# Result additions in four pieces and row picks a group ahead, in a two-block transformer kernel

## The reference

```python
gates = jnp.sum(jax.nn.one_hot(eidx, N_EXPERTS, dtype=jnp.float32) * w[..., None], axis=-2)
hg = jnp.einsum('cd,edf->cef', xc, w_eg)
hu = jnp.einsum('cd,edf->cef', xc, w_eu)
a = jax.nn.silu(hg) * hu * gch[..., None]
routed = jnp.einsum('cef,efd->cd', a, w_ed)
shared = (jax.nn.silu(t @ w_sg) * (t @ w_su)) @ w_sd
x = x + gate2 * (routed + shared)
```

## Time and profile before

| | |
|---|---|
| median of 3 runs | 1175.13 us (1171.66 to 1176.56) |
| the profiled execution | 1178.99 us |
| its span | 1177.2 us |
| TensorE busy | 1006.8 us (86%) |
| VectorE busy | 449.6 us (38%) |
| transfers | 376.77 MB, mean 320 GB/s |
| mean granted TensorE clock | 0.931 of full |

### The profile page before, as it was taken

How to read it: one execution, slowest core, us unless ns; L and a number is a source line. 1 busy time by engine, 2 the same in 40 slices (tenths; PEclk the granted TensorE clock), 3 DMA queues, 4 the chain that set the end, 5 groups by cost and what they waited for, 6 DMA issues and landing times. The chain is left out here.

```text
span 1177.2 us, 14285 instructions
## 1 busy us (share of the span) xinstructions
PE 1006.8 (86%) x5213; PEld 573.7 (49%) x5213; DVE 449.6 (38%) x1011; ACT 207.2 (18%) x438; POOL 157.7 (13%) x209
## 2 busy tenths in 40 slices
PE   6999997987977767799999998889999999837286
PEld 3545543444322222345555444858878888403231
DVE  1795272244211110234915116544443433234431
ACT  2204201330111111302624112010111111100000
POOL 0000011100000000000000000045554554221000
PEclk9999998898999999699999998899999999978597
DMA  8552588989799999952598959779999999998886
GB/s 320 207 214 73 197 315 313 358 366 388 304 421 423 422 421 416 345 143 90 200 343 312 360 211 372 283 276 409 375 381 353 357 373 343 377 417 355 364 334 272
DMA packets 71813, 376.77 MB, mean 320 GB/s; under 512 B 20047, under 2 KB 22347, under 8 KB 41883
## 3 DMA queue, kind: packets, MB, share of 16 engines
q1 hardware_dynamic: 58347, 328.54, 71.6%
q0 software_dynamic: 13424, 47.69, 10.5%
HBM read 338.66 MB, written 48.14 MB: 329 GB/s over the span
## 5 line engine op out<-in xcount | busy, mean ns | idle before, releaser
L877 PE MATMUL bank<-wring,hT 128*128 128x512 f32 (+3 forms) x608 | 249.8, 570 | 7.7 <-DVEq L1704 3.8
L877 PEld LDWEIGHTS bank<-wring,hT 128*128 128x128 f32 x608 | 112.9, 198 | 132.5 <-issue 122.0
L1112 PEld LDWEIGHTS bank<-qT,wring 128*128 128x128 f32 x1408 | 158.9, 192 | 5.3 <-issue 4.3
L1112 PE MATMUL bank<-qT,wring 128*128 128x128 f32 x1408 | 159.3, 275 | 0.2 <-DVE qT L2253 0.2
L1040 PE MATMUL bank<-wring,kT 128*32 128x512 f32 x768 | 102.6, 665 | 39.4 <-DMA wring<-in_w_pack 36.9
L1002 PE MATMUL bank<-kT,x 128*128 128x128 f32 x480 | 72.0, 321 | 51.9 <-DVEq L1704 51.5
L1002 PEld LDWEIGHTS bank<-kT,x 128*128 128x128 f32 x480 | 69.3, 234 | 63.0 <-DVEq L1704 55.4
L788 POOL DMA_INDIRECT PRT<-xn_parts_dram,part_now x88 | 89.6, 1019 | 39.0 <-issue 22.7
L1126 PE MATMUL bank<-wring,PRT 128*128 128x512 f32 x176 | 77.7, 593 | 0.9 <-ACT hT L1429 0.7
L1040 PEld LDWEIGHTS bank<-wring,kT 128*32 128x32 f32 x768 | 26.2, 120 | 106.6 <-issue 57.5
L877 PE MATMUL bank<-wring,yT 128*128 128x512 f32 x160 | 70.2, 595 | 0.7 <-ACT yT L1429 0.7
(11 more groups left out here) (368 smaller groups left out, 1005.3 us busy)
## 6 DMA issues: line engine op xcount, KB each, us to landing
wring<-in_w_pack SPq DMA_DIRECT2D x154, 1024.0 KB, 14.6
wring<-in_w_pack SPq DMA_DIRECT2D x22, 2048.0 KB, 8.8
y_dram<-gateB SPq DMA_DIRECT2D x8, 4096.0 KB, 19.5
wring<-in_w_ada POOLq DMA_DIRECT2D x24, 1024.0 KB, 7.3
wring<-in_w_pack SPq DMA_DIRECT2D x32, 512.0 KB, 15.3
wring<-in_pack_z.0 SPq DMA_DIRECT2D x1, 2048.0 KB, 10.9
wring<-in_pack_z.2 SPq DMA_DIRECT2D x1, 2048.0 KB, 17.3
wring<-in_pack_z.3 SPq DMA_DIRECT2D x1, 2048.0 KB, 8.9
```

The costliest lines, as they stand in the source:

```text
L877: mm = nc.tensor.matmul(b[:, 0:n], lhs(k, t), w[:, k, c0:c0 + n], start=(k == 0), stop=(k == nk - 1))
L1112: mm = nc.tensor.matmul(bank[:, s, f * P:(f + 1) * P], item_gate_up(s)[:, k, f * P:(f + 1) * P], xT[:, s, k, :], start=(k == 0), stop=(k = ...
```

## The change

It has four parts. In block two VectorE weighs and picks one group further ahead: `weigh(1)` and `pick(2)` come before the steps, and `step(i)` is now hidden, next_rows, gated_result, `weigh(i+1)`, `pick(i+2)`. The sixteen result additions are cut into four pieces of four, one after each of steps 1, 2 and 3, and the fourth after the loop, ahead of the last group's hidden product; the closing pair of a token half comes with pieces 1 and 3 (counted from 0). Since three steps are now written out, the least number of groups in block two is 5. And on TensorE the last group of each block makes down half 1 and down half 0 one behind the other, then both sums; the other groups keep their order.

```diff
+LEAST_SMALL_QUADS = 5
...
-                    for half in (1, 0):
-                        if half == 0 and last is None:
-                            pe.wait_ge(E(f"moe{n}_quad_rows_copied"), i + 1)
+                    def down(half):
                         if last is not None:
                             pe.wait_ge(E(f"moe{n}_last_loaded{4 + half}"), 64)
...
+                    def combined(half):
                         if half == 1:
                             pe.wait_ge(E(f"moe{n}_quad_half_copied"), i)
...
+                    down(1)
+                    if last is None:
+                        combined(1)
+                        pe.wait_ge(E(f"moe{n}_quad_rows_copied"), i + 1)
+                        down(0)
+                    else:
+                        down(0)
+                        combined(1)
+                    combined(0)
...
                 def step(i):
-                    weigh(n, i)
-                    pick(n, i + 1)
+                    if n == 1:
+                        weigh(1, i)
+                        pick(1, i + 1)
                     hidden(i)
                     next_rows(i)
                     if n == 2:
                         gated_result(i)
+                        weigh(2, i + 1)
+                        pick(2, i + 2)
...
-                    for t in range(2):
-                        step(t + 1)
-                        add_results(t)
-                with dve.Fori(n + 1, quads_n) as i:
-                    step(i)
-                weigh(n, quads_n)
-                hidden(quads_n)
-                if n == 2:
+                    weigh(2, 1)
+                    pick(2, 2)
+                    for c in range(3):
+                        step(c + 1)
+                        add_results(c)
+                    with dve.Fori(4, quads_n) as i:
+                        step(i)
+                    add_results(3)
+                    hidden(quads_n)
                     gated_result(quads_n)
...
-            def add_results(t):
-                for k in range(TAKES[2]):
-                    q = t * TAKES[2] + k
-                    dve.wait_ge(E(f"moe2_results_fetched{q % 4}"), 16 * (q // 4 + 1))
-                    o = shared[:, t, :]
+            def add_results(c):
+                t = c // 2
+                for q in range(4 * c, 4 * c + 4):
+                    dve.wait_ge(E(f"moe2_results_fetched{q % 4}"), 16 * (c + 1))
+                    o, k = shared[:, t, :], q - TAKES[2] * t
...
+                if c % 2 == 1:
+                    dve.wait_ge(E("moe2_rows_added"), (t + 1) * TAKES[2])
+                    link(V.tensor_tensor(shared[:, t, :], shared[:, t, :], gateB[:, 1, :], ALU.mult))
+                    link(V.tensor_tensor(shared[:, t, :], x[:, t, :], shared[:, t, :], ALU.add))
```

More of the change, by code:

```diff
@@ L449, in quad_count @@
         def quad_count(engine, n):
-            least = FIXED_QUADS if n == 1 else 4
+            least = FIXED_QUADS if n == 1 else LEAST_SMALL_QUADS
             return engine.value_load(pairs_n[0:1, 1:2], min_val=least, max_val=QUADS[n])
         def last_quad(engine, n):
-            least = FIXED_QUADS if n == 1 else 4
+            least = FIXED_QUADS if n == 1 else LEAST_SMALL_QUADS
             return engine.value_load(pairs_n[0:1, 2:3], min_val=least - 1, max_val=QUADS[n] - 1)
@@ L1953, in tile_starts @@
                 link(V.tensor_scalar(pairs_f, pairs_f, 3.0, None, ALU.max))
-                link(V.tensor_scalar(quads_f, quads_f, 4.0, None, ALU.max))
+                link(V.tensor_scalar(quads_f, quads_f, float(LEAST_SMALL_QUADS), None, ALU.max))
                 V.tensor_scalar(pairs_n[0:1, 2:3], quads_f, 1.0, None, ALU.subtract)
@@ L2220, in quads @@
                     next_rows(1)
-                else:
-                    for t in range(2):
-                        step(t + 1)
-                        add_results(t)
-                with dve.Fori(n + 1, quads_n) as i:
-                    step(i)
-                weigh(n, quads_n)
-                hidden(quads_n)
-                if n == 2:
+                    with dve.Fori(2, quads_n) as i:
+                        step(i)
+                    weigh(1, quads_n)
+                    hidden(quads_n)
+                else:
+                    weigh(2, 1)
[4 more added lines that the diff above has]
+                    with dve.Fori(4, quads_n) as i:
+                        step(i)
+                    add_results(3)
+                    hidden(quads_n)
                     gated_result(quads_n)
@@ L2316, in add_results @@
                     V.scalar_tensor_tensor(o, yg[:, q % 4, :], share_large[:, t, k:k + 1], o, ALU.mult, ALU.add).then_inc(E("moe2_rows_added"), 1)
-                dve.wait_ge(E("moe2_rows_added"), (t + 1) * TAKES[2])
-                link(V.tensor_tensor(shared[:, t, :], shared[:, t, :], gateB[:, 1, :], ALU.mult))
-                link(V.tensor_tensor(shared[:, t, :], x[:, t, :], shared[:, t, :], ALU.add))
+                if c % 2 == 1:
+                    dve.wait_ge(E("moe2_rows_added"), (t + 1) * TAKES[2])
+                    link(V.tensor_tensor(shared[:, t, :], shared[:, t, :], gateB[:, 1, :], ALU.mult))
+                    link(V.tensor_tensor(shared[:, t, :], x[:, t, :], shared[:, t, :], ALU.add))
             link(V.memset(gates[:], 0.0))
```

## The result

| | before | changed |
|---|---|---|
| median (runs) | 1174.40 us (4) | 1160.77 us (4; 1159.09 to 1162.37) |
| ratio | | 0.9885, 95% interval 0.9856 to 0.9914 |
| profiled execution, span | 1178.99, 1177.2 us | 1162.37, 1160.5 us |
| mean granted TensorE clock | 0.931 | 0.944 |

The change makes the kernel 13.6 us faster by the medians. The forecast was 1158, so 17 us less than the 1175.13 it started from: the time lies inside the range of 1151 to 1168, 2.8 us above the forecast.

What follows compares the result with a forecast made beforehand. The prediction took block two's four-slab stage as bound by transfers with two holes. Savings of 14.5 + 1.5 + 1.0 = 17.0 us from the 1175.13 us median gave 1158 us, range 1151 to 1168.

Steps and rivals of the forecast that it cites:

- Two holes, 14.5 us, and not 41 of waits: Block two's four-slab stage: only two gaps in transfers count, 14.5 us, not TensorE's 41.4 us of waits on VectorE.
- Pieces hide behind waits for weights: VectorE, block two: each four-addition piece fits in a wait for weights; uncovered it costs 5.1 us, or 7.6 with closing pair.
- The queue never runs dry, 10 us in hand: SyncE's weight loads, block two, groups 3 to 5: each is issued 10 us or more before the queue would empty.
- Ends of the bytes: Block two's stage: closing the holes saves 14.5 us, bounded by 13.3 and by nothing beyond the bytes still to move.
- TensorE's order, 1.5 and 1.0 us: Last group: both down halves ahead of both sums save 1.5 us in block two, 1.0 in block one.
- Picks ahead: VectorE, block two: weighing and picking a group ahead, priced together with the addition pieces at 14.5 us.
- The first rival, the clock: Block two, groups 3 to 5: half clock makes TensorE the bound, slower at 1188 us by the median; chance 0.05.

Runs made afterwards that it cites:

- e1: Changed kernel with the result additions again in two blocks of eight, picks ahead and TensorE's new order kept: 1166.38 us, ratio 0.9943.
- e5: Changed kernel without the sixteen gathers and sixteen result additions: 1142.60 us, ratio 0.9713.
- e6: Kernel before the change, without the sixteen gathers and sixteen result additions: 1142.56 us, ratio 0.9722.
- e7: Changed kernel with all gathers, but each result addition on only 8 of 1024 columns: 1159.33 us, ratio 0.9858.
- e9: Changed kernel run once more, unaltered, on the same chip as e10 to e12: 1161.43 us, ratio 0.9903.
- e3: Kernel before the change with only TensorE's new order in the last group of each block: 1172.00 us, ratio 0.9974.
- e8: Changed kernel with TensorE's old order and three dummy products ahead of block two's last gate and up quarter, keeping the clock up: 1162.20 us, ratio 0.9878.
- e4: Changed kernel with TensorE's old order in the last group, VectorE's new order kept: 1162.30 us, ratio 0.9908.
- e10: Same kernel as e4, run again beside e9 on one chip: 1163.05 us, ratio 0.9909.
- e12: Kernel before the change with only the additions in four pieces, weigh, pick and TensorE's order old: 1162.25 us, ratio 0.9894.
- e11: Changed kernel with the last group's first third of weights issued only after the previous group's down products: 1172.85 us, ratio 0.9994.

## Why the prediction was right

- *Two holes, 14.5 us, and not 41 of waits.* Right. No stretch of five microseconds from 1010 to 1145 is under 400 GB/s. e1 has three quarters of the waits and a hole of 7.0 us, e5 and e6 show the bytes as the price. My reading of the bytes per slice had left out a slice at 417 GB/s, and the waits on weights grew to 35 us where I had 15 to 25.
- *Pieces hide behind waits for weights.* Right (e7). The pieces end 2.3 us ahead of the hidden product of group 2, where I had 1, and 3.0 ahead of group 5's, where I had 4.
- *The queue never runs dry, 10 us in hand.* Right in kind. The down weights were issued at 1062, 1092 and 1129 where I had 1057, 1093 and 1126. The first is late because I took the 16.8 us of the earlier trace rows, the median of four loads, for the time of all four: by the landing records the last of them landed 24 us behind the first issue before and 26 in the changed kernel, where TensorE waited 6.0 us for it.
- *Ends of the bytes.* Here the sum was 2.7 us too high by this profile and 1.2 by e9's. I had counted bytes as if the 16 transfer engines were one: "nothing beyond the bytes, since all of them still have to move". The holes of before had also levelled them, and what counts is the slowest. The work that follows saw 11.8 us of the 14.5 (13.3 in e9). I had also taken the holes from an execution 3.9 us above the median and subtracted them from the median; e3's stretch was 2.8 us shorter. How the 3.4 us between 17.0 and 13.6 divide, the runs don't tell.
- *TensorE's order, 1.5 and 1.0 us.* Over-sized: 0.5 to 1.0 us in block two and 0 to 0.8 in block one by the traces, 1.6 together by the medians. I took the weights as in for block two at 1165.5; the last landing record of before is at 1165.93, and with the change down half 0 waits for them. For block one I assumed nearly so, and there it waits 1.69 us.
- *Picks ahead.* I gave the whole stage one price. The pieces would have done alone; the 3.4 us of steps fit in the wait that is there anyway.
- *The first rival, the clock.* Wrong here. The granted clock over the stage rose, 0.81 to 0.89. It did fall to half in the waits of 6.0 and 7.6 us, and not in one of 3.8. The Trainium skill, page "TensorE: Matmul & The Clock Gate", section "HAM oscillation — how this bites in real kernels", says that such a loop starts cold in every pass; here it was some thirds of a group, not all. Within the stage the transfers hid it (418 GB/s over the stretch); in the tail it cost 1.1 to 4 us (e8 against e4, e10 and e12).
- That the profiled spans differ by 16.7 us, so near the 17.0, is in part luck: 2.8 us of it come from block one, mostly from the clock's return (over 480 to 484 it is 0.50 in the trace before and 1.00 in the other; there it was 0.56 already from 476 to 480, before the new order had acted).

## What to carry to other kernels

Where an engine waits long, look first at whether the transfers stood still with it: only the microseconds in which they did can be won, and the rest of the wait is hidden behind bytes. Long side work (here ten operations in a row) belongs in pieces no longer than the wait that is there anyway; which order the short steps around it have matters little. When a stage becomes bound by transfers, work that ends before the last landing gains nothing from a faster clock or an earlier place; what ends behind it, 8.7 to 12.6 us here, still pays for the clock. Whether the new order and a full clock together end sooner still wasn't run.

## What the runs showed of the hardware

The 16 transfer engines don't finish together. Some 30 to 40 us behind a hole (before, e1, e3, e11) the share falls within 1 to 2 us; with the queue full throughout the fall takes 3 to 4 us without gathers and 4 to 5 with them. The last 16 landing records of the weights then lie 2.3 to 3.6 us apart, against 0.7 before, and the work waits for the slowest: 1.2 and 2.7 us in two profiles of one kernel. A hole levels them: the loads issued at 1043 and 1078, ahead of the first hole of before and behind it, lie 3.2 and 0.9 us apart. Where the difference comes from stays open. Whether rows left out of the gathers (the choices that belong to slabs) load the engines unequally wasn't tried.
